# Expert tiles of two halves of 64 slots in two column groups

## The reference, cut to what matters

```python
def hier_moe(x, w_rg, b_rg, w_re, b_re, w_gate, w_up, w_down):
    g_logits = (x @ w_rg).astype(jnp.float32) + b_rg.astype(jnp.float32)
    g_idx = jnp.argmax(g_logits, axis=-1)
    ...
    top_p, top_i = lax.top_k(e_prob, TOP_K)
    gate = p_g * top_p / jnp.sum(top_p, axis=-1, keepdims=True)
    eid = g_idx[..., None] * EXPERTS_PER_GROUP + top_i
    combine = jnp.sum(jax.nn.one_hot(eid, N_EXPERTS, dtype=jnp.float32) * gate[..., None], axis=-2)
    h = jax.nn.silu(jnp.einsum('btd,edf->btef', x, w_gate)) * jnp.einsum('btd,edf->btef', x, w_up)
    return jnp.einsum('btef,efd->btd', h * combine[..., None].astype(h.dtype), w_down)
```

## Time and profile before

| | us |
|---|---|
| median of 3 executions | 1899.7 |
| lowest and highest | 1898.5, 1909.7 |
| the profiled execution | 1910.1 |
| its span, first to last instruction | 1908.0 |
| first gate product to last gate product's first record | 1573.9 to 1863.8 |
| end of the last add to the running sum | 1888.0 |

### The profile page before, as it was taken

The page is one execution under the profiler, slowest core; times in us unless marked ns, Lnnn a source line. Parts: engine busy times, 40 slices in busy tenths (PEclk is TensorE's granted clock), DMA queues, the critical chain, the costliest instruction groups (busy, mean ns, idle before and its releaser), DMA issues. The chain is left out here.

```text
span 1908.0 us, 22057 instructions
## 1 busy us (share of the span) xinstructions
PE 1623.8 (85%) x7437; PEld 1100.0 (58%) x7438; DVE 712.9 (37%) x1496; ACT 454.9 (24%) x1062; POOL 256.2 (13%) x454
## 2 busy tenths in 40 slices
PE   5999889975898989897477799999989829999993
PEld 3565556655465655565345588888768724444441
DVE  4258676676254544444222311211142241111210
ACT  2233333222243433333122301101033200111110
POOL 1000101010222222221322000000000001222211
PEclk8999999997899999998788899999989959999997
DMA  7001200000302020000775212111054284989754
GB/s 220 1 1 56 68 1 24 1 24 0 97 1 58 1 58 1 25 1 24 260 280 169 78 34 67 33 34 34 2 161 125 100 291 122 309 233 272 230 143 126
DMA packets 135879, 179.44 MB, mean 94 GB/s; under 512 B 9427, under 2 KB 106758, under 8 KB 135702
## 3 DMA queue, kind: packets, MB, share of 16 engines
q1 hardware_dynamic: 123126, 132.05, 21.8%
q0 software_dynamic: 12608, 44.05, 8.6%
q10 hardware_dynamic: 48, 2.10, 0.3%
HBM read 147.30 MB, written 35.32 MB: 96 GB/s over the span
## 5 line engine op out<-in xcount | busy, mean ns | idle before, releaser
L946 PE MATMUL psum<-branch_part,kept 128*128 128x384 f32 (+1 forms) x576 | 202.8, 508 | 1.2 <-DVE branch_part L1177 1.2
L2175 PE MATMUL psum<-moe_part,kept 128*128 x416 | 185.9, 600 | 5.9 <-issue 4.4
L946 PEld LDWEIGHTS psum<-branch_part,kept 128*128 128x128 f32 (+1 forms) x576 | 108.9, 194 | 77.4 <-issue 18.4
L480 PE MATMUL psum<-kept,branch_part 128*128 128x368 f32 x384 | 125.5, 483 | 10.1 <-PEq L223 5.1
L1605 PE MATMUL psum<-kept,merge_part 128*128 128x368 f32 x384 | 125.6, 481 | 9.7 <-DMA merge_part<-w_da_out 9.7
L1611 PE MATMUL psum<-split 128*128 128x368 f32 x384 | 133.3, 347 | 0.0
L2175 PEld LDWEIGHTS psum<-moe_part,kept 128*128 128x128 f32 x416 | 77.7, 192 | 95.7 <-issue 95.1
L485 PE MATMUL psum<-branch_part,kept 128*128 128x512 f32 (+1 forms) x288 | 126.3, 593 | 1.3 <-DVE kept L666 1.3
L1612 PE MATMUL psum<-split 128*128 128x368 f32 x384 | 126.9, 331 | 0.0
L1613 PE MATMUL psum<-split 128*128 128x368 f32 x384 | 126.6, 330 | 0.0
L1660 DVE TENSOR_TENSOR merge_part<-merge_part,psum 128x368 f32<-128x368 f32 x48 | 23.6, 534 | 254.3 <-ACT merge_part L1636 254.3
(11 more groups left out here) (320 smaller groups left out, 2670.5 us busy)
## 6 DMA issues: line engine op xcount, KB each, us to landing
branch_part<-cache_k SPq DMA_DIRECT2D x64, 256.0 KB, 6.0
branch_part<-cache_v POOLq DMA_DIRECT2D x64, 256.0 KB, 5.1
moe_part<-w_gate SPq DMA_DIRECT2D x16, 1024.0 KB, 8.0
moe_part<-w_up SPq DMA_DIRECT2D x16, 1024.0 KB, 13.1
moe_part<-w_down SPq DMA_DIRECT2D x16, 1024.0 KB, 14.0
branch_part<-w_in SPq DMA_DIRECT2D x8, 1024.0 KB, 8.0
merge_part<-w_in SPq DMA_DIRECT2D x16, 512.0 KB
branch_part<-w_in SPq DMA_DIRECT2D x12, 512.0 KB
```

Of the source, the lines that this page charges most:

```text
L480: mm = pe.matmul(bank[:, 0:CH], Wb[0][:, k, c0:c0 + P], K["xT"][:, k, CH * i:CH * i + CH], start=(k == 0), stop=(k == KC - 1))
L946: mm = pe.matmul(bank_of(("z", h, i))[:ROWS[i], 0:384], K["xT"][:, k, cols(i)], Wb[h % 2][:, k, :], start=(k == 0), stop=(k == KC - 1))
L2175: mm = pe.matmul(psum[:, 2 + par, :], XT[par][:, k, :], K["GU"][:, bass.ds(KC * b + k, 1), :], start=(k == 0), stop=(k == KC - 1))
```

## The change

A tile still has 128 slots, but now it is two halves of 64, and each half has an expert of its own. Experts fill halves, not tiles. `SLOTS` (tiles provided for) falls from 34 to 26, and `K["expert"]` and `K["buffer"]` have two entries a tile.

- On PE each product becomes two of 64 columns of the array: lower half of the slots with the weights of the first half's expert from its load buffer, upper half with those of the second half's expert from a fixed double buffer, `GU2[par]` and `Wd2[par]`.
- ACT and DVE copy the second half's weights there for every step: ACT chunks 0 to 5 of gate and up (`copy_gate`, two copies of 128 x 1536), DVE chunks 6 and 7 (`copy_up`, 128 x 1024) and the down weights (`copy_down`, 128 x 2048). Each waits until the expert of the second half is announced.
- POOL adds a tile's result by two indirect DMAs of 64 rows, one after the other.
- In routing a second list of 64 lanes is made by 18 more products, and the end of an expert in steps is its end in halves, divided by two and rounded up.

```diff
-SLOTS = (2 * TOK - E) // P + E + 1
+GROUPS = 2
+GROUP = P // GROUPS
+ENTRIES = (2 * TOK - 2) // GROUP + E
+SLOTS = -(-ENTRIES // (2 * GROUPS)) * 2
...
+CUT = 6
...
-                    mm = pe.matmul(psum[:, 2, 0:2 * SLOTS], lane[:rows, n, :], what[:rows, n, :], start=(n == 0), stop=(n == 2 * NT - 1))
+                    pe.matmul(psum[:, 2, 0:2 * SLOTS], lane[:rows, n, :], what[:rows, n, :], start=(n == 0), stop=(n == 2 * NT - 1))
+                    mm = pe.matmul(psum[0:64, 3, 0:SLOTS], lane[:rows, n, 64:128], what[:rows, n, 0:SLOTS], start=(n == 0), stop=(n == 2 * NT - 1))
...
-            dve.tensor_copy(K["dest"], empty)
+            dve.tensor_copy(K["dest"][0:64, 0, :], empty[0:64])
+            dve.tensor_copy(found[0:64], psum[0:64, 3, 0:SLOTS])
...
+            dve.tensor_scalar(ends, incl, 1.0 / GROUPS, 0.5 - 0.5 / GROUPS, ALU.mult, ALU.add)
...
+            dve.tensor_copy(K["ends"], ends)
...
+        def second_of(e, j):
+
+            x = e.value_load(K["expert"][0:1, bass.ds(2 * j + 1, 1)], min_val=0, max_val=E - 1)
+            b = e.value_load(K["buffer"][0:1, bass.ds(2 * j + 1, 1)], min_val=0, max_val=BUFFERS - 1)
+            e.wait_ge(weights_ready, x + 1)
+            return b
...
-                            pool.wait_ge(y_out[par], 16 * (j // 2 - 1))
-                        add_rows(K["dest"][:, j - 3:j - 2], 1 - par)
+                            pool.wait_ge(y_out[par], 32 * (j // 2 - 1))
+                        add_rows(K["dest"][0:64, 0, j - 3:j - 2], 1 - par, 0)
+                        pool.wait_ge(y_out[1 - par], 32 * ((j - 3) // 2) + 16)
+                        add_rows(K["dest"][0:64, 1, j - 3:j - 2], 1 - par, 1)
...
             def down(j, par, first, b):
                 pe.wait_ge(ht_done, j + 1)
+                pe.wait_ge(down_copied, j + 1)
...
-                        mm = pe.matmul(psum[:, 5 + n, :], hT[par][:, k, :], K["Wd"][:, bass.ds(2 * b + k, 1), 512 * n:512 * n + 512], start=(k == 0), stop=(k == 1))
+                        pe.matmul(psum[0:64, 5 + n, :], hT[par][:, k, 0:64], K["Wd"][:, bass.ds(2 * b + k, 1), 512 * n:512 * n + 512],
+                                  start=(k == 0), stop=(k == 1))
+                        mm = pe.matmul(psum[64:128, 5 + n, :], hT[par][:, k, 64:128], Wd2[par][:, k, 512 * n:512 * n + 512],
+                                       start=(k == 0), stop=(k == 1))
...
+                pe.wait_ge(gate_copied, j + 1)
+                pe.wait_ge(up_copied, j + 1)
                 for k in range(KC):
-                    mm = pe.matmul(psum[:, 2 + par, :], XT[par][:, k, :], K["GU"][:, bass.ds(KC * b + k, 1), :], start=(k == 0), stop=(k == KC - 1))
+                    pe.matmul(psum[0:64, 2 + par, :], XT[par][:, k, 0:64], K["GU"][:, bass.ds(KC * b + k, 1), :],
+                              start=(k == 0), stop=(k == KC - 1))
+                    mm = pe.matmul(psum[64:128, 2 + par, :], XT[par][:, k, 64:128], GU2[par][:, k, :],
+                                   start=(k == 0), stop=(k == KC - 1))
...
+            def copy_gate(j, par, first=False):
+                b = second_of(act, j)
+                if not first:
+                    act.wait_ge(gu_done, j - 1)
+                for k in range(0, CUT, 3):
+                    ins = act.activation(GU2[par][:, k:k + 3, :], K["GU"][:, bass.ds(KC * b + k, 3), :], ACT.Copy)
+                ins.then_inc(gate_copied, 1)
...
                 with act.If(i < last):
+                    copy_gate(2 * i + 2, 0)
                     silu(2 * i + 1, 1)
                     result(2 * i, 0, i)
                     hidden(2 * i + 1, 1)
+                    copy_gate(2 * i + 3, 1)
                     silu(2 * i + 2, 0)
...
                 with dve.If(i < last):
+                    copy_up(2 * i + 2, 0)
                     hidden(2 * i + 1, 1)
                     place(2 * i + 2, 0, False)
                     result(2 * i, 0, i)
+                    copy_down(2 * i + 2, 0)
+                    copy_up(2 * i + 3, 1)
                     hidden(2 * i + 2, 0)
                     place(2 * i + 3, 1, False)
                     result(2 * i + 1, 1, i)
+                    copy_down(2 * i + 3, 1)
```

More of the change, by code:

```diff
@@ L55 @@
 BUFFERS = 4
-FEWEST = -(-2 * TOK // P)
+FEWEST = -(-2 * TOK // P) // 2 * 2
 LEVELS = [64, 32, 16, 8, 4, 2, 1]
@@ L202, in build @@
         K["X"] = [sb(D) for _ in range(2)]
-        K["expert"], K["buffer"], K["token"], K["dest"], K["ends"], K["before_last"] = (sb(n).bitcast(I32) for n in (SLOTS, SLOTS, SLOTS, SLOTS, E, 1))
+        K["expert"], K["buffer"], K["token"], K["dest"], K["ends"], K["before_last"] = (x.bitcast(I32) for x in (sb(2 * SLOTS), sb(2 * SLOTS), sb(SLOTS), sb(2, SLOTS), sb(E), sb(1)))
         K["slot_weight"] = sb(SLOTS)
+        K["Wd2"], K["Y"] = [sb(2, D) for _ in range(2)], [sb(D) for _ in range(2)]
         top[0] = 0
@@ L1862, in phase_route @@
         M, pre, tot = sb(NT, E), sb(NT, E), sb(E, NT)
-        inc, cmp9, ntile, incl, excl, sm = sb(E, NT), sb(E, NT), sb(E), sb(E), sb(E), sb(NT, E)
-        lt, eid, eidb, step, last = sb(SLOTS, E), sb(SLOTS), sb(SLOTS), sb(SLOTS), sb(1)
+        inc, over, ntile, incl, excl, sm = sb(E, NT), sb(E, NSTEP), sb(E), sb(E), sb(E), sb(NT, E)
+        lt, eid, eidb, step, last, ends = sb(GROUPS * SLOTS, E), sb(GROUPS * SLOTS), sb(GROUPS * SLOTS), sb(GROUPS * SLOTS), sb(1), sb(E)
         sl, tile, within, tok1, spare = sb(2, NT), sb(2, NT), sb(2, NT), sb(NT), sb(1)
@@ L2031, in _ @@
             dve.tensor_copy(K["expert"], eid)
-            dve.tensor_copy(K["ends"], incl)
-            dve.tensor_tensor(step[:, 0:SLOTS // 2 - 1], consts[:, 15:13 + SLOTS:2], incl[:, E - 1:E].to_broadcast([P, SLOTS // 2 - 1]), ALU.is_lt)
+            dve.tensor_scalar(ends, incl, 1.0 / GROUPS, 0.5 - 0.5 / GROUPS, ALU.mult, ALU.add)
+            D_()
+            dve.tensor_scalar(ends, ends, ROUND, None, ALU.add)
+            D_()
+            dve.tensor_scalar(ends, ends, -ROUND, None, ALU.add)
+            D_()
+            dve.tensor_copy(K["ends"], ends)
+            dve.tensor_tensor(step[:, 0:SLOTS // 2 - 1], groups[:, 2 * GROUPS::2 * GROUPS], incl[:, E - 1:E].to_broadcast([P, SLOTS // 2 - 1]), ALU.is_lt)
             D_()
@@ L2105, in _, with add_rows @@
         def _(pool):
-            def add_rows(rows, par):
-                pool.indirect_dma_start(out=K["sum_dram"], out_offset=bass.IndirectOffsetOnAxis(ap=rows, axis=0),
-                                        in_=Y[par], in_offset=None, compute_op=ALU.add).then_inc(y_out[par], 16)
+            def add_rows(column, par, half):
+                pool.indirect_dma_start(out=K["sum_dram"], out_offset=bass.IndirectOffsetOnAxis(ap=column, axis=0),
+                                        in_=Y[par][64 * half:64 * half + 64, :], in_offset=None, compute_op=ALU.add).then_inc(y_out[par], 16)
             def pair_of_tiles(i):
@@ L2133, in _ @@
                 pool.wait_ge(y_dve, 2 * last + n + 1)
-                pool.wait_ge(y_out[1 - n % 2], 16 * last + 16 * (n == 1))
+                pool.wait_ge(y_out[1 - n % 2], 32 * last + 32 * (n == 1))
                 pool.tensor_tensor(spare[:, n + 1:n + 2], K["half"][:, 0:1], K["half"][:, 0:1], ALU.add)
-                add_rows(dest_end[:, n + 1:n + 2], n % 2)
+                add_rows(dest_end[0:64, 0, n + 1:n + 2], n % 2, 0)
+                pool.wait_ge(y_out[n % 2], 32 * last + 16 - 32 * (n == -1))
+                pool.tensor_tensor(spare[:, n + 4:n + 5], K["half"][:, 0:1], K["half"][:, 0:1], ALU.add)
+                add_rows(dest_end[0:64, 1, n + 1:n + 2], n % 2, 1)
         @block.tensor
@@ L2219, in _ @@
             hidden(1, 1)
+            copy_gate(3, 1)
             silu(2, 0)
@@ L2252, in result, with copy_up, copy_down @@
                 if i is not None:
-                    dve.wait_ge(y_out[par], 16 * i)
+                    dve.wait_ge(y_out[par], 32 * i)
                 dve.tensor_copy(Y[par][:, 512:], psum[:, 6, :]).then_inc(y_dve, 1)
+            def copy_up(j, par, first=False):
+                b = second_of(dve, j)
+                if not first:
+                    dve.wait_ge(gu_done, j - 1)
+                dve.tensor_copy(GU2[par][:, CUT:KC, :], K["GU"][:, bass.ds(KC * b + CUT, KC - CUT), :]).then_inc(up_copied, 1)
+            def copy_down(j, par, first=False):
+                b = second_of(dve, j)
+                if not first:
+                    dve.wait_ge(y_made, j)
+                dve.tensor_copy(Wd2[par], K["Wd"][:, bass.ds(2 * b, 2), :]).then_inc(down_copied, 1)
+            copy_up(0, 0, True)
             place(0, 0, True)
+            copy_up(1, 1, True)
+            copy_down(0, 0, True)
             hidden(0, 0)
             place(1, 1, True)
+            copy_down(1, 1, True)
+            copy_up(2, 0)
             hidden(1, 1)
@@ L2262, in _ @@
             result(0, 0, None)
+            copy_down(2, 0)
+            copy_up(3, 1)
             hidden(2, 0)
```

43 lines of the change are left out of this document (28 added, 15 removed).

## The result

| | before | after |
|---|---|---|
| median us, 4 executions each on one chip | 1901.8 | 1928.1 |
| lowest and highest | 1898.5, 1909.7 | 1924.6, 1934.8 |
| ratio, 95% interval | | 1.014 (1.012 to 1.016) |
| the profiled execution | 1910.1 | 1924.6 |
| its span | 1908.0 | 1923.0 |

The change makes the kernel 1.4% slower. 1928 is inside the range of 1885 to 1950, 19 us above the 1909 forecast, 3 us outside the forecast's own range of 1893 to 1925, and on the side that had 0.37, not the one that had 0.54.

A forecast was written before the change was run, and what follows sets the result against it. TensorE (PE), busy 85% of the span, was taken to bound the kernel. From first product to last step -14.8, routing +10.5, tail +7.7, lateness +6 gave +9.4 us, so 1909; own range 1893 to 1925, whole range 1885 to 1950.

The forecast's parts named there:

- routing, list to first gate product: In routing, +8.2 us for PE's list and +2.3 for DVE's added work, all on the path: +10.5.
- steps 0 and 1: First two steps of the experts' loop: 12.3 and 11.65 us before, 0.56 more each, 25.1 together.
- step 4: Experts' loop, the step behind the second long one: 12.0 us plus 2.1 for the slower clock, 14.1.
- the rest up to the last step: Experts' loop behind step 4: sixteen steps of 12.0 and two skipped iterations at 1.65 us, plus 6 for lateness.
- from the last step to the last landing: End of the experts' phase: half adds of 5.2 us one after another take 31.9 us, +7.7.
- The new step: Experts' loop on PE: pairs at no additional time, four changes of grouping at 0.14 us, 12.0 us a step.
- Rivals 1 and 2: On PE: pairs don't run side by side, +227 us, chance 0.04; weight loads stand in the open, +116, chance 0.03.
- The two long steps: Steps 2 and 3: copies ahead of silu wait for experts 3 and 4, announced after the next load's issue; 19.8 and 22.3 us.
- The clock's share: On PE after each long step's idle gap, 6.5 us in step 2: slower clock adds 2.1 us to the next step.
- rival 3: On POOL, half adds become the bound and pace the loop: +41 us, 1950, deciding from about 6 a half; chance 0.15.
- The small lateness: In the experts' loop, late gathers behind half adds and borderline announcements of experts 5, 11, 14, 15: +6 us (0 to +20).
- rival 4: In steps 2 and 3, the two announcement waits are short or hidden: 20 us less, 1889; chance 0.13.

The follow-up runs named there:

- one_add: The changed kernel with one indirect add of 128 rows a tile, to consecutive rows, instead of two of 64: 1899.4 us, ratio 0.998 to before.
- perm_five: The changed kernel with experts in order 0, 4, 8, 12, 1, ..., one add a tile, one routing list, five load buffers: 1874.4 us, ratio 0.986 to before.
- Wait_only: The changed kernel, second half's weights copied in steps 0 and 1 only, ACT's wait for the announcement kept ahead of silu: 1913.9 us, ratio 1.007 to before.
- announce: The changed kernel with SP announcing expert e - 1, not e - 2, ahead of the wait and load of expert e: 1911.2 us, ratio 1.005 to before.
- five: The changed kernel with five load buffers for experts instead of four: 1912.2 us, ratio 1.003 to before.
- copies_once: The changed kernel with second halves' weights copied in steps 0 and 1 only, without later announcement waits on ACT and DVE: 1897.2 us, ratio 1.000 to before.
- gather_early: The changed kernel with the gather of the next X issued between a tile's two half adds, not behind them: 1927.3 us, ratio 1.014 to before.
- after_again: The changed kernel unaltered, run once more on the chip of wait_only, five and list_apart: 1926.9 us, ratio 1.010 to before.
- list_apart: The changed kernel with routing's list products grouped, nine of 128 lanes then nine of 64, instead of alternating: 1924.0 us, ratio 1.010 to before.

## Why the prediction came out as it did

The two profiled executions differ by 14.5 us (their spans by 15.0), where the sum said 9.4. By its own steps, the profile of after beside it:

| term | forecast | measured |
|---|---|---|
| routing, list to first gate product | +10.5 | +7.1 (31.0 for 23.9) |
| steps 0 and 1 | 25.1 | 23.9 |
| step 2 | 19.8 | 23.3 |
| step 3 | 22.3 | 23.8 |
| step 4 | 14.1 | 13.9 |
| the rest up to the last step | 193.9 + 6 | 206.6 |
| from the last step to the last landing | 31.9 | 32.1 |

These come to 16.5 us against before; the copy of the sums behind them took another half, and the phases ahead were 2.1 us shorter.

**The new step** was right: 12.0 forecast, 11.99 and 12.01 measured wherever nothing else holds it, so the pairs are free and the four changes of grouping cost 0.14 each. Rivals 1 and 2 fell with it. One small term of the loop was misread: before skips four iterations at its end, not three, and after two; in one_add and perm_five these two cost 0.8 us, where 1.65 stood.

**The two long steps** were right in place and mechanism. Wait_only shows that it is the wait, announce that the first is SP's order. The second is SP's order too, as the prediction had it: the data of expert 4 were there by 1628 us, the announcement came at 1642, behind the issue of the load of expert 5. Announce shows that without the first wait the load itself would have been late there, and five that an earlier load takes both away. Their size was short by 4.7 us in all, 3.5 of it in step 2: I took 1.52 us for issuing the down weights from the earlier trace rows, and here it took 4.00; the sixteen such issues of before's trace take 1.1 to 5.7, and I had read one. The clock's share was right. PE in order of time behind the gap of step 2 (the granted clock is 0.50 from 1626.07 to 1628 and 1.00 from 1631 on):

```profile
1626.07 1.11 PE L2215 MATMUL psum<-moe_part,kept 128*64 x1 [1.94 <-issue]
...
1627.82 1.06 PE L2215 MATMUL psum<-moe_part,kept 128*64 x1
...
1628.68 1.06 PE L2215 MATMUL psum<-moe_part,kept 128*64 x1
...
1630.49 0.59 PE L2215 MATMUL psum<-moe_part,kept 128*64 x1
...
1630.92 0.59 PE L2215 MATMUL psum<-moe_part,kept 128*64 x1
```

Pairs come 0.86 us apart at first (1.2 GHz) and 0.43 later (2.4 GHz); about five late pairs are 2.1 us.

**Routing** was 3.4 us too dear. The list grew by 9.2 (forecast 8.2) and DVE's part behind it by 2.1 (2.3), both as worked out. Wrong was the step "all of it is on the path", read from a gap of 5 us between DVE's end and the next phase in the earlier trace rows. After, DVE's last row and, at once behind it, the chain's first of the phase:

```profile
1573.41 0.19 DVE L2068 CAST moe_part<-kept 128x52 int32<-128x52 f32 x1
```

```profile
1574.26 0.06 issue
```

Of the gap of 5.0 us 0.7 is left (before, the chain enters the phase at 1569.44). So it was no fixed delay but slack, and 4.4 us of the growth went into it. What filled it before was a transfer: POOL's second gather of X rows, issued at 1560.40, with this many us to landing (the last number):

```profile
moe_part<-normed,moe_part POOLq DMA_INDIRECT x1, 8.2
```

It landed at 1568.6, and the phase's first product (turning X) came 1.8 us later. In after the second gather is issued at 1567.45 and lands in 5.6 us, at 1573.1, ahead of DVE's end at 1573.60, and the first product comes 1.65 us behind that. In all thirteen profiles the phase's first product starts 1.6 to 1.8 us behind the last of three: DVE's end, this landing, SP's last issue. No run was made to test this, but the profiles hold both cases. The landing stands in the trace of before, so this term could have been worked out ahead. The phase's start then took 0.2 us more: 9.2 + 2.1 - 4.4 + 0.2 = 7.1.

**The small lateness** is the step that failed. I gave +6 to the adds in the loop, thinking of a late gather in some steps, and kept "the adds become the bound" as rival 3 at 0.15, deciding "from about 6 us a half on average". They average 6.2. So rival 3 is what happened, in a mild form: in copies_once, five, gather_early and after the chain is adds for 56 to 89% of the stretches read above, and where a tile has one add (one_add, perm_five) they are off it. From the terms it cost 12.7 us where 6 stood (13.7 against the 192.9 us that one_add needs for the same sixteen steps), not the 41 of the rival (by its own terms 53: 40 halves at two thirds 8.4 and one third 5.2 are 293 us, not 281), because I had put a half under load at 8.4 us most of the time, and of the 22 halves in that stretch eleven took 4.6 to 5.4 and only eight 7.6 to 8.8. The lone 4.7 was below my 5.2; what decided the mean were the ones that met a load. What could have told it: 2 x 5.2 and the issues are 11.4 us, 0.6 under the step, so that anything above it in any step is passed on, never regained, since each add waits for the one before. I weighed the lateness of single steps where I should have compared two chains.

**What stays open.** Medians differ by 26 us, profiles by 14.5. List to end accounts for 17 to 18.5 (375.0 and 376.3 against 358.0 and 357.8). The remaining 8 or so of the medians would have to be in the phases ahead, which the change does not touch. There the start of the list scatters between 1534.5 and 1554.8 us over the profiles of all kernels. The scatter lies mostly in two phases, the recurrence (438 to 449 us) and the prompt attention (420 to 436), while merge and output together take 471 to 472 us in every profile, and it goes roughly with the mean granted clock: 0.93 ahead of the list in the two earliest (wait_only, copies_once), 0.92 in the latest (after_again), and over single executions of before 0.930 at 1894.4 us and 0.921 at 1909.0. Which of the two follows from the other no run tells. Whether the changed kernels have a systematic share in it, no run settles. The same holds for perm_five, whose median fell by 10 us less than its list to end.

**The chances.** Half of rival 4's and most of the forecast's weight stood within 1%. The result was 1.4% because of the adds' 7 us, step 2's 3.5, and these open 8. That the terms' sum came within 8 us of list to end's growth of 17 is partly luck: routing was 3.4 us too dear and the first two steps 1.2, and that hid the long steps' 4.7.

## What to carry to other kernels

When a serial chain of transfers runs beside the engine that bounds a loop, compare the chain's mean per step with the step, under the load of the loop, before anything else: here one that fitted by 5% on paper did not fit. Splitting an indirect add in two cost nearly a second one here (4.7 and 4.7 for 5.9 us), so look first for a layout (here an order of the experts) in which it needn't be split. And a wait inserted ahead of unrelated work in an engine's queue has the price of everything behind it; it is read off by asking when its last signal is given, not how long its own work is.

## What the runs showed of the hardware

- Two products of 64 columns in the two halves of the array, each with its own new weight load, start within 10 ns of each other and cost what one product of 128 columns did: 0.43 us a pair of 512-column records, over 352 pairs.
- A change between products on all 128 columns and products on 64 costs 0.14 to 0.15 us, measured twice: four in each step (12.0 for 11.45), and 32 fewer in list_apart (4.9 us).
- An indirect add of 64 rows of 4 KB lands in 4.7 us alone where 128 rows take 5.9; it keeps POOL for 1.42 us where the larger one takes 1.59. Beside weight loads the halves take 4.6 to 8.8.
- SP's issue of an expert's down weights, 1 MB, took 1.5 to 5.6 us within one execution of after. The kernel before shows the same, of which I had read one. Two of its rows, SP in order of time:

```profile
1633.08 5.37 SPq L2061 DMA_DIRECT2D moe_part<-w_down  x1
1644.67 5.74 SPq L2061 DMA_DIRECT2D moe_part<-w_down  x1
```

What the queue waits for there, no run tells.
